# Other slots for the filling pieces in the RWKV phases of a two-block transformer kernel

## What is computed

```python
def wkv7_scan(r, w, k, v, a, b):
    def step(state, inp):
        r_t, w_t, k_t, v_t, a_t, b_t = inp
        sa = jnp.einsum('bhvk,bhk->bhv', state, a_t)
        state = (state * w_t[:, :, None, :] + sa[..., None] * b_t[:, :, None, :]
                 + v_t[..., None] * k_t[:, :, None, :])
        return state, jnp.einsum('bhvk,bhk->bhv', state, r_t)
```

## Time and profile before

| | |
|---|---|
| time, median of 3 runs | 1293.83 us (1291.23 to 1294.66) |
| time of the profiled execution | 1295.59 us |
| its span | 1293.4 us |
| busy: TensorE, VectorE, ScalarE, GpSimd | 97%, 69%, 52%, 18% |
| TensorE's granted clock | full in all 40 slices |

### The profile page before, as it was taken

The page is one execution under the profiler, slowest core; times in us unless marked ns, Lnnn a source line. Parts: engine busy times, 40 slices in busy tenths (PEclk is TensorE's granted clock), DMA queues, the critical chain, the costliest instruction groups (busy, mean ns, idle before and its releaser), DMA issues.

```text
span 1293.4 us, 26528 instructions
## 1 busy us (share of the span) xinstructions
PE 1259.0 (97%) x10000; PEld 1130.5 (87%) x10000; DVE 898.2 (69%) x1758; ACT 669.6 (52%) x1281; POOL 238.8 (18%) x358
## 2 busy tenths in 40 slices
PE   7999999999999999999999989999999999999997
PEld 6989999889999989999889977888888976888886
DVE  6778888658675667878646566777746676777744
ACT  5465555444366546676445366443335575534432
POOL 0012222221354201333302000122100000111200
PEclk9999999999999999999999999999999999999999
DMA  8321122124411354545555412544554622455452
GB/s 348 115 99 67 67 68 99 35 98 168 159 66 67 115 196 147 195 169 187 196 195 192 155 66 98 196 175 182 195 195 163 206 92 95 165 194 189 175 193 93
DMA packets 27059, 189.95 MB, mean 147 GB/s; under 512 B 2993, under 2 KB 3249, under 8 KB 4817
## 3 DMA queue, kind: packets, MB, share of 16 engines
q1 hardware_dynamic: 25920, 182.61, 39.2%
q0 software_dynamic: 1040, 5.96, 1.6%
HBM read 186.47 MB, written 1.05 MB: 145 GB/s over the span
## 4 chain that ended last, share of the span: by engine, by line
PE 86%; DVE 5%; ACT 5%; DVEq 1%; issue 1%; DMA 1%; POOL 1%; POOLq 0%; ACTq 0%; SPq 0%
PE ps L617 33%; PE ps L565 14%; PE ps L678 12%; PE ps L680 6%; PE ps L932 3%; PE ps L590 1%; PE ps L771 1%; DVE w_lo L2102 1%; PE ps L597 1%; PE ps L949 1%; PE ps L1023 1%; DVE ring_r L2089 1%; PE ps L1033 1%; PE ps L832 1%; ACT xn L1483 1%
## 5 line engine op out<-in xcount | busy, mean ns | idle before, releaser
L1541 ACT ACTIVATE w_hi<-ring 128x1024 fp32r<-128x1024 f32 x125 | 132.7, 1062 | 295.6 <-PE ps L617 156.6
L2102 DVE TENSOR_TENSOR w_lo<-ring,w_hi 128x1024 fp32r<-128x1024 f32 x125 | 153.2, 1225 | 128.1 <-ACT w_hi L1541 127.9
L678 PE MATMUL ps<-h_both,w_hi 128*128 128x512 f32 x672 | 237.7, 399 | 0.0
L680 PE MATMUL ps<-h_both,w_lo 128*128 128x256 f32 x672 | 188.7, 281 | 0.0
L617 PE MATMUL ps<-h_both,w_hi 128*128 128x256 f32 x912 | 165.7, 284 | 0.8 <-DVE w_lo L2108 0.8
L2108 DVE TENSOR_TENSOR w_lo<-ring,w_hi 128x1024 fp32r<-128x1024 f32 x125 | 159.6, 1277 | 0.0
L678 PEld LDWEIGHTS ps<-h_both,w_hi 128*128 128x128 f32 x672 | 126.3, 188 | 31.5
L565 PE MATMUL ps<-oT_r,ring_r 128*128 128x256 f32 x512 | 144.1, 282 | 0.0
L617 PEld LDWEIGHTS ps<-h_both,w_hi 128*128 128x128 f32 x912 | 142.5, 192 | 1.4 <-DVE w_lo L2108 1.2
L1546 ACT ACTIVATE w_hi<-ring 128x1024 fp32r<-128x1024 f32 x125 | 131.0, 1048 | 0.0
L617 PE MATMUL ps<-h_both,w_lo 128*128 128x256 f32 x456 | 129.0, 283 | 0.0
(11 more groups left out here) (442 smaller groups left out, 2943.8 us busy)
## 6 DMA issues: line engine op xcount, KB each, us to landing
ring<-in_weights SPq DMA_DIRECT2D x170, 1024.0 KB, 4.8
arena<-in_aux POOLq DMA_DIRECT2D x1, 2112.0 KB, 13.5
grow<-in_rows POOLq DMA_DIRECT2D x3, 512.0 KB, 4.7
cst<-in_consts SPq DMA_DIRECT2D x1, 1497.5 KB, 18.5
x<-in_x SPq DMA_DIRECT2D x2, 512.0 KB, 4.6
arena<-in_swbias POOLq DMA_DIRECT2D x1, 1024.0 KB, 10.7
arena<-arena POOLq DMA_DIRECT2D x1, 1024.0 KB, 9.1
out<-xn SPq DMA_DIRECT2D x4, 256.0 KB, 2.2
```

What stands on the lines that cost most here:

```text
L678: pe.matmul(bank[:].rearrange("p (a t) -> p a t", a=2), hi, h_both[:, :, k, :], start=k == 0, stop=False)
L680: m = pe.matmul(bank[:, 0:S], lo, h_hi[:, k, :], start=False, stop=k == KT - 1)
L1541: act.activation(w_hi[:, half_of(u0, m), WH:], ring[:, (u0 + m) % RING, WH:], ACT.Copy).then_inc(w_hi_p, 1)
L2102: dve.tensor_tensor(w_lo[:, half_of(u0, m), WH:], ring[:, (u0 + m) % RING, WH:], w_hi[:, half_of(u0, m), WH:].bitcast(F32), ALU.subtract). ...
```

## The change

One table is added and used in the phases that have none of their own (n = -1 to 4). Instead of one piece at the end of every slot and two in slot 5, two pieces stand at the end of slots 1, 3 and 9, three in slot 5, one in slots 7, 8, 10 and 11, none in 0, 2, 4 and 6. The extra piece ahead of power 0 stays. Both ways make 13 behind the slots' work and 14 in all.

```diff
+            PIECES = {1: 2, 3: 2, 5: 3, 7: 1, 8: 1, 9: 2, 10: 1, 11: 1}
+
             def rwkv_phase(n):
 ...
-                    for _ in range((2 if slot == 5 else 1) if pieces is None else pieces.get(slot, 0)):
+                    for _ in range((PIECES if pieces is None else pieces).get(slot, 0)):
                         next(fill, None)
```

## The result

Eleven runs of each: 1297.0 us (1296.53 to 1297.6) with the change, 1294.66 (1291.23 to 1295.43) before it. The ratio is 1.0021 (95% interval 1.0014 to 1.0029), so the kernel became slower by 0.21%, some 2.7 us, and a ratio of 1 lies outside the interval. The profiled execution took 1297.15 us against 1295.59.

The account below looks back on a forecast made before the run. TensorE, busy for 97% of the span, was taken as the bound. Phases 0 to 4 add 3 x 0.51 + 0.71 + 0.61 = 2.85 us, taking the median from 1293.83 to 1296.7 us, range 1293.4 to 1299.2.

Parts of the forecast that it names:

- The wait in slot 8: TensorE reaches L1041, scan_state of chunk 2, early and waits 0.71 us for u from ScalarE.
- Borders: Tile changes beside the powers: 0.10 us before a piece against 0.11 before a scan product, taken as 0.
- The state in slot 3: VectorE's state of chunk 1 is just ready when L1023 follows power 1: 0, between -0.02 and 0.05 us in phase 0.
- Slots 1 and 5: Results needed ahead of the pieces in these slots are ready before TensorE asks for them: 0.
- Given back at the grams: End of slot 11: old waits for VectorE's last z are swallowed, 0.20 us in phase 3, 0 in phase 1, 0.10 in phase 0.
- Phase -1: A longer wait before power 4 delays the rest by 0.7 us, swallowed by the 0.66 us wait before the grams: 0.
- the second rival: VectorE's list in slots 9 to 11 sets the grams, or ScalarE's row begins earlier; loss 0 to 1 us; 13%.
- That end can't move: ScalarE's L1714 delivers u for slot 8 at 181.54, after a gapless row from 178.29 started by piece 8.

Follow-up runs that it names:

- the pair in slot 7: The changed kernel with the piece that had moved to slot 9 put in slot 7 instead; ratio 1.0002 of before the change (0.9993 to 1.0012).
- the shorter row: The changed kernel with ScalarE's gate_key ahead of take_rk instead of behind it; 1296.29 us, 1.0011 of before the change.
- piece 8 earlier: Kernel before the change: TensorE's gate_key behind slot 5's pieces, ScalarE's high_half ahead of gate_key, VectorE's low_half ahead of add_z; ratio 0.9988.
- the piece back in slot 6: The changed kernel with one piece taken from slot 9 back to slot 6, behind power 3; ratio 1.0001 of before the change (0.9991 to 1.0011).

## Why the prediction was right

- **The wait in slot 8** (0.71 us): 0.70. L1041 starts 0.80 us behind the last matmul of the piece, of which 0.12 are there without a wait, and it takes 0.32 us to L1043 instead of the 0.30 of before. Counted from the start of phase 3, L1043 stands at 18.35 us in both kernels (181.93 - 163.58 and 184.35 - 166.00): ScalarE's row took 3.25 us as said, its start did not move, and TensorE arrives there with one piece less done.
- **Borders** (0): 0. L1033 behind power 3 takes 0.32 us (182.10 to 182.42), 0.33 was taken. The experiment with the pair in slot 7 has the same four moved borders and the phases of before. One reading was off without harm: a piece behind a 128x128 product isn't free of a border, it takes 0.79 instead of 0.72 us behind L898 (180.83 to 181.62 in the earlier trace rows); both kernels have equally many of these.
- **The state in slot 3** (0, at most 0.05 in phase 0): in phase 0 TensorE's L1023 starts at 84.39, where power 1 ends, and takes 0.33 us to L1024, the plain price behind a power. VectorE had the state at 84.30, 0.09 us ahead of L1023; a product that does wait, as L1041 in slot 8, starts 0.05 us behind the end of its producer (183.98 to 184.03). So nothing was late, by some 0.04 us in phase 0.
- **Slots 1 and 5** (0): phases 2 to 4 leave nothing over for them.
- **Given back at the grams** (0.20, 0 and 0.10 us): the distance is 0.21 in phases 0 to 4 now, so the old waits were swallowed in full. The prediction had VectorE's z not moving, and it ends 24.74 us into phase 3 before the change and 24.75 with it. Phase 3 was to get 0.51 us longer and got 0.53.
- **Phase -1** (0): the wait ahead of power 4 went from 0.40 to 1.10 us, and the grams start 0.27 us behind the last piece instead of 0.94. With 0.21 as the distance without a wait, the wait is down from 0.73 (0.66 in the bracket) to 0.06. From its `low_rank` to the next phase it is 24.77 us in both kernels.

```profile
68.14 0.34 PE L932 MATMUL ps<-arena 64*64 64x64 f32 x8 [1.10 <-ACT arena L1710]
...
73.79 0.28 PE L565 MATMUL ps<-oT_r,ring_r 128*128 128x256 f32 x1
74.06 0.35 PE L932 MATMUL ps<-arena 64*64 64x64 f32 x9
```

The sum was 2.85 us and is 2.94. Of the 0.09 us, 0.05 come from the prediction's sum taking 0.71 us a phase where its own text has everything from slot 9 on 0.72 later. The medians say 2.3 us, the ratio 2.7 (1.8 to 3.8 by its interval); the difference to the phases is within what the runs scatter. That the median, 1297.0, lies only 0.3 above the 1296.7 forecast is partly luck: the median of before over eleven runs is 0.8 higher than the one over three that was reckoned from, and the difference of the medians is 0.5 smaller than the sum.

Two statements beside the sum need mending. The reasoning on the grams took VectorE's last z to stand "at the end of a row of its own work without a gap", and the second rival spoke of "VectorE's list in slots 9 to 11", as if that list stood fixed. But the row starts with a wait for TensorE, in the trace of before already:

```profile
182.13 0.58 DVE L2362 SCALAR_TENSOR_TENSOR arena<-ps,arena 64x64 f32<-64x64 f32 x2 [0.36 <-PE ps L1041]
```

The experiments with the shorter row and with piece 8 earlier agree. On the kernel before the change, with ScalarE having u earlier, L1041 starts as before (18.04 us into phase 3) and is done 0.08 us sooner, `take_state` starts 0.09 us sooner (18.46 instead of 18.55 us into the phase), the last z ends 0.05 us sooner (24.69 instead of 24.74), and the wait ahead of the grams stays. In the changed kernel both readings give the same number, since L1041 did not move: `take_state` starts at 18.56. And "That end can't move" was true for the change alone: ScalarE idles 2.4 us ahead of `take_rk`, and `gate_key`'s 0.31 us fit in there.

## What to carry to other kernels

Filling work that keeps an engine busy is also the cover of whatever comes back from another engine, so moving it costs the part of that cover that had no slack (here 0.70 us for a piece of 0.72), less what a later wait of the same engine swallows (0.20 of it in three phases); look for the place with 0.1 us of slack, not at the average. Where a wait ends last on an in-order engine, its order is worth trying before its amount of work: here, with the pieces as the change has them, two moves in ScalarE's program took phases 0 to 4 from 146.9 to 143.6 us, and the best place of the pieces that was tried took them to 144.0 without a move on ScalarE. And where a wait seems to belong to a partner's long list, see whether that list itself starts at a result of the engine that waits.

## What the runs showed that I had not expected

The same wait of 2.0 us on TensorE, near 768 us, is followed by about 3.4 us at 1.2 GHz in one execution and by none in another, and that alone makes 1.6 us, over half of what this change is worth. All eleven kernels have the wait (2.00 to 2.02 us) in their profiled executions; in eight a stretch at 1.2 GHz begins at its end or up to 1.3 us behind it, and in three (the changed kernel, the one with the piece back in slot 6 and the one with ScalarE's row made shorter) none does. What decides it is open. They also come to phase -1 between 52.2 and 53.4 us, and one has the pause of 0.6 us in phase -1. Phases 0 to 4 do not differ by more than 0.03 us where the order is the same. For a change of this size the phase in the trace is the finer scale.
